# Seven quarter products in the last two groups of two down projections

## The reference

```
u = einsum('bsd,df->bsf', rms_norm(x, ffn_norm_w), w_up)
u = conv_b + sum(conv_w[j] * shifted(u, j) for j in range(3))
gate, val = split(u)                       # 2816 channels each
x = x + einsum('bsf,fd->bsd', silu(gate) * val, w_down)
```

## Time and profile before

| | |
|---|---|
| runs | 1334.34, 1334.60, 1336.63 us; median 1334.6 |
| the profiled execution | 1336.37 us; span 1334.6 us |
| granted clock of TensorE | 0.999 of full |
| busy PE / PEld / DVE / ACT / POOL | 1314.2 / 1147.7 / 1005.9 / 713.7 / 107.0 us |
| DMA | 155.59 MB, mean 117 GB/s |
| instructions | 19065 |

### The profile page before, as it was taken

How to read it: one execution, slowest core, us unless ns; L and a number is a source line. 1 busy time by engine, 2 the same in 40 slices (tenths; PEclk the granted TensorE clock), 3 DMA queues, 4 the chain that set the end, 5 groups by cost and what they waited for, 6 DMA issues and landing times. The chain is left out here.

```text
span 1334.6 us, 19065 instructions
## 1 busy us (share of the span) xinstructions
PE 1314.2 (98%) x7406; PEld 1147.7 (86%) x7406; DVE 1005.9 (75%) x1254; ACT 713.7 (53%) x1018; POOL 107.0 (8%) x82
## 2 busy tenths in 40 slices
PE   9999999999999999999999999999999999999997
PEld 6889888879989989989999898788888888888886
DVE  7898999999989689647749769997567636753663
ACT  4424888774546345534546856797355314431444
POOL 0000000002100591000012001010200000000002
PEclk9999999999999999999999999999999999999999
DMA  9634411157333433232342251401222232232212
GB/s 366 258 122 111 158 63 47 36 217 288 129 136 104 143 141 127 95 99 92 111 174 72 71 166 48 114 6 64 95 95 94 95 98 92 94 121 100 73 69 79
DMA packets 28730, 155.59 MB, mean 117 GB/s; under 512 B 3248, under 2 KB 5680, under 8 KB 15600
## 3 DMA queue, kind: packets, MB, share of 16 engines
q1 hardware_dynamic: 28656, 154.58, 33.4%
HBM read 145.39 MB, written 4.19 MB: 112 GB/s over the span
## 5 line engine op out<-in xcount | busy, mean ns | idle before, releaser
L2096 DVE TENSOR_TENSOR w_lo<-raw,w_hi 128x2048 fp32r<-128x2048 f32 (+3 forms) x135 | 249.0, 1846 | 59.1 <-ACT w_hi L1220 46.2
L1220 ACT ACTIVATE w_hi<-raw 128x2048 fp32r<-128x2048 f32 (+2 forms) x78 | 138.9, 1780 | 85.9 <-PE psum L647 62.7
L647 PE MATMUL psum<-h_hi,w_hi 128*128 128x512 f32 x360 | 92.5, 395 | 0.8 <-DVE w_lo L2096 0.6
L647 PE MATMUL psum<-h_hi,w_lo 128*128 128x512 f32 x360 | 91.1, 391 | 0.0
L647 PE MATMUL psum<-h_lo,w_hi 128*128 128x512 f32 x360 | 90.4, 389 | 0.0
L647 PE MATMUL psum<-xg_lo,w_hi 128*128 128x512 f32 x336 | 83.0, 389 | 0.0
L647 PE MATMUL psum<-xg_hi,w_lo 128*128 128x512 f32 x336 | 83.0, 389 | 0.0
L647 PE MATMUL psum<-xg_hi,w_hi 128*128 128x512 f32 x336 | 83.0, 389 | 0.0
L647 PEld LDWEIGHTS psum<-h_lo,w_hi 128*128 128x128 f32 x360 | 67.6, 188 | 14.1
L647 PEld LDWEIGHTS psum<-h_hi,w_hi 128*128 128x128 f32 x360 | 66.0, 188 | 15.4 <-issue 1.6
L647 PEld LDWEIGHTS psum<-h_hi,w_lo 128*128 128x128 f32 x360 | 67.0, 188 | 13.7
(11 more groups left out here) (476 smaller groups left out, 3208.9 us busy)
## 6 DMA issues: line engine op xcount, KB each, us to landing
raw<-w_ffn_in SPq DMA_DIRECT2D x22, 1024.0 KB, 4.9
raw<-w_up SPq DMA_DIRECT2D x22, 1024.0 KB, 4.8
ada_first<-ada SPq DMA_DIRECT2D x16, 512.0 KB, 11.9
raw<-w_gate SPq DMA_DIRECT2D x8, 1024.0 KB, 5.1
raw<-w_mix_out SPq DMA_DIRECT2D x8, 1024.0 KB, 4.9
raw<-w_ffn_out SPq DMA_DIRECT2D x8, 1024.0 KB, 4.9
raw<-w_down SPq DMA_DIRECT2D x8, 1024.0 KB, 4.8
ada_x<-ada SPq DMA_DIRECT2D x11, 512.0 KB, 5.2
```

Of the source, the lines that this page charges most:

```text
L647: last = mm(ps, w[slot][:, k, t * P:(t + 1) * P], part(xv, k0 + k), start=first, stop=final)
L1220: A(w_hi[slot][:, 0:stage.kc, :], raw[slot][:, 0:stage.kc, :], ACT.Copy).then_inc(sem["w_hi_done"], 1)
L2096: return tt(out_lo, full, high.bitcast(F32), ALU.subtract)
```

## The change

Groups 2 and 3 of down0 and down1 are computed as folded groups; groups 0 and 1 stay plain. The gated product is kept in `product` (in the room of `h_hi`) instead of the two buffers `up_p`, and after the last chunk VectorE makes four sums of its quarters there, in place; their parts go to `down_t`, `down_lo` and, for the quarter used last, to B12 of `mid_hi` and `mid_lo`. The regions lie in banks of their own (`DOWN_BANK`). What was written out by `run` is now a list by hand on ScalarE and on VectorE (`down_folded`), in which the additions to `x` are by quarters. TensorE runs `gemm` for groups 0 and 1 and then `folded`. down2 is as before.

```diff
-FOLDS = {"ffn_in0": 4, "ffn_in1": 0, "ffn_in2": 0}
+FOLDS = {"ffn_in0": 4, "ffn_in1": 0, "ffn_in2": 0, "down0": 2, "down1": 2}
 FOLD_BANK = [(0, 1, 5, 4), (2, 3, 6, 7)]
+DOWN_BANK = [(4, 0, 1, 5), (6, 2, 3, 7)]
...
-            for p in (0, 5) if name.startswith("down") else (5, 4):
+            for p in (7, 6, 5) if name.startswith("down") else (5, 4):
-PAIR_SUMS, DOWN_SUMS, DOWN_PARTS = 3, 15, 5
+DOWN_SUMS, DOWN_PARTS = 4, 4
...
-    up_p = [at(f"up_p{s}", 86.5 + 2 * s, [P, S]) for s in range(2)]
+    product = nc.alloc_sbuf_tensor_at("product", [P, DC, S], F32, offset=h_at)
+    down_lo = nc.alloc_sbuf_tensor_at("down_lo", [P, DC, S], F32R, offset=h_at)
+    down_t = [nc.alloc_sbuf_tensor_at("down_t1", [P, 4, S // 2], F32R, offset=h_at + 28 * 1024)[:, :, :]
+              ] + [at(f"down_t{n}", kb, [P, 4, S // 2], F32R)[:, :, :] for n, kb in ((2, 72), (3, 76))]
+    down_ext = [[nc.alloc_sbuf_tensor_at(f"down_{part}0", [P, 3, 4, P], dt, offset=h_at + kb * 1024), at(f"down_{part}1", kb1, [P, 3, 4, P], dt)]
+                for part, kb, kb1, dt in (("hi", 16, 82.5, F32R), ("low", 22, 88.5, F32R), ("f", 22, 88.5, F32))]
...
                     elif p == 4:
                         pe.wait_ge(sem["t_lo_done"], parts_done)
+                        if name.startswith("down"):
+                            pe.wait_ge(sem["fold_out"], read_count[name, g, 7])
...
-                gemm(st[f"down{r}"], mid_hi, mid_lo, ready=("mid_lo_done", 8 + FC + PART_AT[r], 0), steps=(0, 2 if r < 2 else 1))
+                gemm(st[f"down{r}"], mid_hi, mid_lo, ready=("mid_lo_done", 8 + FC + PART_AT[r], 0), steps=(0, 1))
+                if r < 2:
+                    folded(st[f"down{r}"], (mid_hi, *down_t), (mid_lo, *(block_of(down_lo, b) for b in (B11, B22, B12))),
+                           T_PARTS + DOWN_PARTS * (r + 1))
...
                 return evac
+
+            def down_folded(stage, r):
+
+                split_hi(stage, 1, 1, 0)
+                for n, (dst, b) in enumerate(zip((down_t[0], down_t[2], down_t[1]), (B11, B12, B22))):
+                    act.wait_ge(sem["t_sum"], T_SUMS + DOWN_SUMS * r + n + 1)
+                    A(dst, block_of(product, b), ACT.Copy).then_inc(sem["t_hi_done"], 1)
+                for _ in fold_highs(stage, 2):
+                    pass
+                highs = fold_highs(stage, 3)
+                next(highs)
+                fold_seed(stage, 2, 1, 2)
+                act.wait_ge(sem["t_sum"], T_SUMS + DOWN_SUMS * (r + 1))
+                A(block_of(mid_hi, B12), block_of(product, B21), ACT.Copy).then_inc(sem["t_hi_done"], 1)
+                fold_seed(stage, 2, 6, 3)
+                next(highs)
+                next(highs)
+                fold_seed(stage, 3, 1, 2)
+                fold_seed(stage, 3, 6, 3)
+                split_hi(stage.next, 0, 0, 0)
...
-                run(st[f"down{r}"], end_squares if r == 2 else (lambda i, s, k, ahead: ahead()))
+                if r < 2:
+                    down_folded(st[f"down{r}"], r)
+                else:
+                    run(st["down2"], end_squares)
...
-                else:
+                elif not name.startswith("down"):
                     dve.wait_ge(sem["tile_done"], 2 * (stage.g0 + k) - 2)
...
-                    tt(up_p[s][:, :], up_a[s][:, :], up_b[s][:, :], ALU.mult).then_inc(sem["mid_f"], 1)
+                    tt(chunk(product, k), up_a[s][:, :], up_b[s][:, :], ALU.mult).then_inc(sem["mid_f"], 1)
                     ahead()
-                    mid_low(DC + FC + c0, k, up_p[s])
+                    mid_low(DC + FC + c0, k, chunk(product, k))
                 return evac
+
+            def down_folded(stage, r):
+
+                name = stage.name
+                quarter = lambda b: block_of(product, b)
+                sums, parts = T_SUMS + DOWN_SUMS * r, T_PARTS + DOWN_PARTS * r
+
+                def plain(k):
+                    for t in range(2):
+                        arrived(stage, k, t)
+                        added = lambda: tt(x[:, 2 * k + t, :], x[:, 2 * k + t, :], bank[2 * k + t], ALU.add)
+                        if t:
+                            free(stage, k, added)
+                        else:
+                            added()
+
+                def add_region(g, c, side, r):
+                    return tt(x[:, 2 * g + c, SIDES[side]], x[:, 2 * g + c, SIDES[side]], region(g, r, True), ALU.add)
+
+                def seventh_and_sixth(g):
+                    dve.wait_ge(sem["fold_mm"], mm_count[name, g, 7])
+                    add_region(g, 1, 1, 4).then_inc(sem["fold_out"], 1)
+                    dve.wait_ge(sem["fold_seed"], seed_count[name, g, 6])
+                    add_region(g, 1, 0, 2).then_inc(sem["fold_out"], 1)
+
+                def fifth(g):
+                    dve.wait_ge(sem["fold_mm"], mm_count[name, g, 5])
+                    dve.wait_ge(sem["fold_out"], read_count[name, g, 7])
+                    add_region(g, 1, 1, 3).then_inc(sem["fold_out"], 1)
+
+                def second(g):
+                    dve.wait_ge(sem["fold_mm"], mm_count[name, g, 2])
+                    add_region(g, 0, 0, 1)
+
+                def last(g):
+                    dve.wait_ge(sem["fold_mm"], mm_count[name, g, 3])
+                    add_region(g, 0, 1, 3)
+                    arrived(stage, g, 1)
+                    dve.wait_ge(sem["fold_out"], read_count[name, g, 6])
+                    free(stage, g, lambda: add_region(g, 1, 0, 4))
+
+                split_lo(stage, 1, 1)
+                dve.wait_ge(sem["mid_f"], DC + PART_AT[r] + DC)
+                for n, (dst, a, b) in enumerate(((B11, B12, B11), (B12, B22, B12), (B22, B22, B11), (B21, B21, B22))):
+                    if n:
+                        dve.wait_ge(sem["t_sum"], sums + n)
+                    else:
+                        dve.wait_ge(sem["mid_hi_done"], DC + FC + PART_AT[r] + DC)
+                        dve.wait_ge(sem["mid_lo_done"], DC + FC + PART_AT[r] + DC)
+                    tt(quarter(dst), quarter(a), quarter(b), ALU.subtract).then_inc(sem["t_sum"], 1)
+                fold_sums(stage, 2)
+                dve.wait_ge(sem["t_sum"], sums + DOWN_SUMS)
+                for n, (hi, b) in enumerate(zip((down_t[0], down_t[2], down_t[1]), (B11, B12, B22))):
+                    dve.wait_ge(sem["t_hi_done"], parts + n + 1)
+                    less(block_of(down_lo, b), quarter(b), hi).then_inc(sem["t_lo_done"], 1)
+                plain(0)
+                fold_lows(stage, 2)
+                fold_last(stage, 2)
+                fold_sums(stage, 3)
+                plain(1)
+                fold_left(stage, 3)
+                seventh_and_sixth(2)
+                dve.wait_ge(sem["t_hi_done"], parts + DOWN_PARTS)
+                less(block_of(mid_lo, B12), quarter(B21), block_of(mid_hi, B12)).then_inc(sem["t_lo_done"], 1)
+                fold_extra(stage, 3)
+                fifth(2)
+                second(2)
+                fold_last(stage, 3)
+                seventh_and_sixth(3)
+                last(2)
+                split_lo(stage.next, 0, 0)
+                fifth(3)
+                second(3)
+                last(3)
```

More of the change, by code:

```diff
@@ L403, in fold_ext @@
         def fold_ext(stage):
-            return fold_hi, fold_lo, fold_f
+            return down_ext if stage.name.startswith("down") else (fold_hi, fold_lo, fold_f)
         def fold_weights(w, ext):
@@ L414, in fold_inputs, with region @@
             return {1: block_of(t, B11), 2: block_of(t, B21), 3: block_of(t, B22), 4: block_of(t, B12), 5: t1, 6: t2, 7: t3}
-        def region(g, r):
-            return bank[FOLD_BANK[g % 2][r - 1]][:, 0:S // 2]
+        def region(g, r, down=False):
+            return bank[(DOWN_BANK if down else FOLD_BANK)[g % 2][r - 1]][:, 0:S // 2]
         mm_count, seed_count, read_count, fold_nth = fold_counts(st)
@@ L905, in product @@
                 def product(g, p):
-                    s, into = g % 2, region(g, {1: 1, 2: 1, 6: 2, 5: 3, 3: 3, 7: 4, 4: 4}[p])
+                    s, into = g % 2, region(g, {1: 1, 2: 1, 6: 2, 5: 3, 3: 3, 7: 4, 4: 4}[p], name.startswith("down"))
                     w = [fold_weights(w_hi[s], ext_hi[s])[p], fold_weights(w_lo[s], ext_lo[s])[p]]
@@ L1249, in fold_seed @@
                     act.wait_ge(sem["group_free"], stage.g0 + g - 1)
-                A(region(g, to), region(g, to - 1), ACT.Copy).then_inc(sem["fold_seed"], 1)
+                down = name.startswith("down")
+                A(region(g, to, down), region(g, to - 1, down), ACT.Copy).then_inc(sem["fold_seed"], 1)
             def split_wide(stage, k, slot, tiles=0):
@@ L2061, in evac @@
                     act.wait_ge(sem["mid_f"], DC + c0 + 1)
-                    A(chunk(mid_hi, k), up_p[s][:, :], ACT.Copy
+                    A(chunk(mid_hi, k), chunk(product, k), ACT.Copy
                       ).then_inc(sem["mid_hi_done"], 1)
                 return evac
+            def down_folded(stage, r):
```

(6 more changed lines are left out.)

## The result

The changed kernel takes 1346.81 us (median of 6 runs, 1345.36 to 1348.14) against 1334.76 for the kernel before (6 runs). The ratio is 1.0084, with a 95% interval of 1.0074 to 1.0094. It is slower, by 9.9 to 12.5 us. The 1346.81 lies 0.3 above the end of the predicted range, 1346.5; taken by the ratio, 1.0084 of the 1334.6 that the prediction starts from is 1345.8, which is inside it. Its profiled execution took 1347.27 us with a span of 1345.2, so 2.1 us lie outside the span, where the kernel before had 1.8.

What follows compares the result with a forecast made beforehand. TensorE matmul time was taken as the bound. Each of two stages was summed as -1.60 + 3.35 + 2.05 + 0.2 = +4.0 us, so +8.0 on 1334.6 gave 1342.6, range 1337.5 to 1346.5.

Steps and rivals of the forecast that it cites:

- The gain on offer: Groups 2 and 3 of down0 and down1: folding gives back 0.80 us a group, 1.60 a stage, 3.20 in all.
- VectorE's list: Fixed work order in each down stage, from group 1's split to the end of `fold_extra(3)`: 26.62 us, never idle.
- The wait at (2,1): Group 2's first folded product on TensorE: 0.8 us late for `fold_left(2)`, contained in the later wait, not added.
- (3,1): Group 3 product wanted five products after (2,1): 1.2 us late for `fold_left(3)`, contained in the later wait, not added.
- (3,7): Group 3 product that needs `fold_extra(3)` from VectorE: starts 3.35 us late in each stage.
- The end of the stage: Late group 3 product waits 2.05 us for `fifth(3)`, queued on VectorE behind the split of up1's first weights.
- The sum: Each down stage: -1.60 + 3.35 + 2.05 + 0.2 = +4.0 us; two stages +8.0.
- The clock: Rival: 12 matmuls behind each of four long TensorE waits run at half speed, 5.8 us more, 1348.4; chance 0.06.
- its own sign: Down stages: a granted clock under 1.00 there would make the prediction wrong.
- slower subtractions on VectorE: Four in-place strided subtractions on the product at 1.78 us each: 2.2 us more a stage, upper end 1347.0.
- Both covers hold: Rival, both stages: VectorE's list is at most 23.4 us and `fifth(3)` comes in time; -3.20, 1331.4; chance 0.05.
- the two single stalls: Rivals, both stages: only the end stall remains, +1.1, 1335.7, chance 0.07; only the list stalls, +3.7, 1338.3, chance 0.07.

Runs made afterwards that it cites:

- experiment 6: Changed kernel with fifth product read before up1's split, three VectorE items put later, product's first sum made behind chunk 6: 1332.83 us, ratio 0.9978 to the kernel before.
- experiment 1: Changed kernel with VectorE reading group 3's fifth product before splitting up1's first weights: 1341.75 us, ratio 1.0044 to the kernel before.
- experiment 2: Changed kernel with three VectorE items, 2.94 us, put behind the low parts that product (3,7) waits for: 1341.13 us, ratio 1.0043 to the kernel before.
- experiment 3: Changed kernel with 16 unused 256-column matmuls between (3,1) and (3,7) in each stage: 1345.48 us, ratio 1.0075 to the kernel before.
- experiment 4: Changed kernel, fifth product read before up1's split, plus 8 or 16 unused matmuls before (3,7): 1340.34 us (1.0034) or 1339.52 us (1.0027).

## Why the prediction was right, and where it was off

*The direction and the bound of the stage.* Right. The gain on offer was put at 0.80 us a group from the pitch of 0.12, and experiment 6 has it: 41.91 against 43.52 us. By the formula of the Trainium skill (TensorE: Matmul & The Clock Gate, "Wait — 56ns, not 53.3ns?") it would have been 1.19 a group and the stage 41.1 us; the measurement, 1.61 us for two groups, decides for the rows.

*VectorE's list.* Right to 0.1 us: 26.62 added up, 26.61 measured, and it was never idle. The wait at (2,1) was given as 0.8 late (0.78), (3,1) as 1.2 late (1.24) and (3,7) as 3.35. Measured against a stall-free stage that started at 1051.00, (3,7) should begin at 1081.40 and began at 1084.67: 3.27. (The working gives 3.33 and, for the end of the stage, 2.07 where 3.35 and 2.05 are written; the two slips cancel.) In-place strided subtractions cost what the same size cost elsewhere, 1.25 us a link (5.00 for four, the last without a follower).

*The end of the stage.* Right. 2.05 was worked out, 2.09 came (1096.99 instead of 1094.90), and experiment 1 shows the cause, as the wait goes with the order of two lines.

*The sum.* The forecast was +4.0 us a stage and the measured stage is +5.42: -1.60, 3.27, 2.09, 0.07 for the first matmul behind the second wait, and 1.59 for products (3,7) and (3,6), which take 2.39 and 2.08 us instead of 1.44 each. Of the 1.59, 0.1 was allowed for as the longer first matmul. The other 1.5, 3.0 in both stages, is the slow stretch, and it agrees with the 1.48 by which the two stages of experiment 1 differ. The forecast had this term at nothing. With it the forecast would have been 1345.6, a ratio of 1.0082 and inside the measured interval.

*The clock* is thus the part of the mechanism that the prediction had wrong, and by its own sign: it said that a granted clock under 1.00 in the stages would make it wrong, and the stages have 0.97. It had named the fall of the clock as a rival, at a chance of 0.06 and with a wrong size: 5.8 us in all for four products at half speed, where 3.0 came. It noted itself that no wait before was longer than 1.3 us, so no row stood behind that low chance. The measured time by the ratio, 1345.8, is 3.2 above the forecast and 2.6 below this rival's 1348.4. That it is inside the range is in part luck: the upper part of the range was there for slower subtractions on VectorE, which did not come, and what filled it was a clock term that the range had no room for by its own reasons.

*The rest*, about 0.3 us, lies outside the span (2.1 against 1.8, to 0.1 in every run of the two). The changed kernel has 19475 instructions instead of 19065. I did not test whether that is the reason.

*The rivals.* "Both covers hold" and the two single stalls are excluded by the rows for (3,7) and (3,3).

What decides whether a wait of 1.8 to 1.9 us is followed by a slow stretch stays open. Of the eight first such waits in a stage (changed kernel, experiments 1 to 3, two stages each) six were followed by one, two were not, with waits of the same length; the two that were not had the same work around them as their partners in the other stage. That it is the idleness that brings the fall is supported by the filled gaps (none of six followed by a slow stretch) and by the stages without waits, but not what tips it in one case and not in another. The second wait of a stage, as it comes in the changed kernel some 6 us behind the end of a slow stretch, was followed by none in two cases, so of all ten waits of this length in the profiles six were followed by one.

## What to carry to other kernels

When matmul work is cut at the price of elementwise work, write out the list of the engine that gets the work from its first start to each instruction that TensorE waits for, by start-to-start distances of the same sizes; this was right to 0.1 us over 26. Busy shares (VectorE had 24.6 of 43.5 us free) don't tell it, since the items have due times: what is needed late is to go behind what is needed early, and a short read that frees a PSUM region goes ahead of a long split for the next stage. Price a TensorE wait of nearly 2 us at its length and up to 1.5 us more for the clock, when matmuls of 256 columns stand behind it; this kernel turned from 0.84% slower to 0.22% faster without any of the added work being removed.

## What the runs showed of the hardware that was not expected

- The granted clock fell to the lower level, 0.50 of full, for about 3.4 us at six of ten waits of 1.8 to 1.9 us. The fall did not come with the idleness but about the time when work began again: 0.4 us behind the start of (3,7) in down0 of the changed kernel and 1.0 behind it in down1, 0.6 in experiment 1, within 0.1 us of the start of (3,3) in experiment 2 and in down0 of experiment 3, and 0.6 behind it in down1 of experiment 3. In the four stages of experiment 4, where no wait was over 0.8 us, there was none in the profiles. The Trainium skill (TensorE: Matmul & The Clock Gate, "The HAM clock gate (the "warmup" mystery)") has two levels and a fall after idleness; the levels agree with the rows, but the waits here are shorter than the idle stretches it warns of, and the measurement decides.
- At the lower level a 256-column matmul had a pitch of 0.213 us (0.85 us for four). At full clock it was 0.12 and not half of that, 0.107, with the weight loads busy all the time. Folding thus gives less than its arithmetic at the full clock, and the lower level costs less than a factor of two.
- Filling a gap with matmuls whose results are not used kept the clock behind the filled place in all six stages where it was done; in the profile of experiment 3 this was worth nothing, as the slow stretch came behind the next wait.
